# Token rows loaded ahead of the last prefetched weight tiles, and narrow products as four 32-token strips

## What is computed

```
# block 1, layer l: the segment ab of the input projection, 4*8 = 32 columns
h = rmsnorm(x, norm_w[l]);  proj = h @ w_in[l]       # ab: decay and gate of the 8 heads
# block 2
x = x + mix @ w_out
hf = rmsnorm(x, g_ffn)
logits = hf @ w_router + b_router                    # 256 x 32
top 4 of 32 per token, gates = softmax of the four
for each expert e, on the rows of its tokens (xb):
    gu = xb @ w_gate_up[e] + b_gate_up[e]            # 1024 x 2048
    g = min(gu[:, :1024], 7);  u = clip(gu[:, 1024:], -7, 7)
    y = ((u + 1) * g * sigmoid(1.702 g)) @ w_down[e] + b_down[e]
x = x + sum of y * gate
gate = sigmoid(rmsnorm(x, g_ple) @ w_ple_gate)
x = x + (p @ w_ple_proj) * gate                      # p: 256 tokens x 256
out = rmsnorm(x, g_final)
```

## Time and profile before

| | us |
|---|---|
| median of three runs | 2119.19 |
| the three runs | 2116.81, 2119.19, 2123.26 |
| the profiled execution, its own time | 2117.58 |
| its span, first to last instruction | 2115.7 |
| TensorE busy | 2011.1 (95%) |
| VectorE busy | 718.4 (34%) |
| ScalarE busy | 449.7 (21%) |
| GpSimdE busy | 100.7 (5%) |

### The profile page before, as it was taken

How to read it: one execution, slowest core, us unless ns; L and a number is a source line. 1 busy time by engine, 2 the same in 40 slices (tenths; PEclk the granted TensorE clock), 3 DMA queues, 4 the chain that set the end, 5 groups by cost and what they waited for, 6 DMA issues and landing times.

```text
span 2115.7 us, 24433 instructions
## 1 busy us (share of the span) xinstructions
PE 2011.1 (95%) x9554; PEld 986.8 (47%) x9554; DVE 718.4 (34%) x2021; ACT 449.7 (21%) x1121; POOL 100.7 (5%) x84
## 2 busy tenths in 40 slices
PE   7999999999999999999996999999999999999998
PEld 6754666445864566544463333333333333333334
DVE  4659565211767666311143111111101111011112
ACT  2151554211143355310121000000000000000003
POOL 0021220000022121000000000000000000000000
PEclk9999999998999999999997999999999999999999
DMA  6643212343453221344816999999999999999993
GB/s 213 251 147 120 81 41 81 120 159 119 145 213 120 83 78 41 119 159 172 305 53 249 387 428 428 427 429 428 429 428 429 428 428 429 427 430 428 429 426 113
DMA packets 103070, 551.17 MB, mean 261 GB/s; under 512 B 9005, under 2 KB 13521, under 8 KB 77906
## 3 DMA queue, kind: packets, MB, share of 16 engines
q1 hardware_dynamic: 101138, 549.57, 64.6%
q10 hardware_dynamic: 1856, 0.57, 0.1%
HBM read 546.90 MB, written 3.21 MB: 260 GB/s over the span
## 4 chain that ended last, share of the span: by engine, by line
PE 75%; DMA 18%; DVE 4%; issue 1%; ACT 1%; SPq 0%; DVEq 0%; ACTq 0%
PE bank L570 26%; PE bank L1111 13%; DMA ring<-w_gate_up_dram 8%; DMA region<-w_gate_up_dram 8%; PE bank L1137 7%; PE bank L856 5%; PE bank L909 3%; PE bank L682 3%; PE bank L1069 2%; PE bank L1055 2%; PE bank L993 1%; PE bank L1103 1%; DMA region<-p_dram 1%; PE bank L766 1%; PE bank L822 1%
## 5 line engine op out<-in xcount | busy, mean ns | idle before, releaser
L1111 PE MATMUL bank<-ring,region 128*64 128x512 f32 x1280 | 288.9, 600 | 16.2 <-DMA ring<-w_gate_up_dram 16.2
L2202 DVE TENSOR_SCALAR region<-bank 128x512 f32<-128x512 f32 x32 | 22.1, 691 | 732.3 <-PE bank L1111 732.3
L570 PE MATMUL bank<-ring,hT 128*128 128x512 f32 (+1 forms) x464 | 194.8, 577 | 0.0
L1111 PEld LDWEIGHTS bank<-ring,region 128*64 128x64 f32 x1280 | 88.1, 138 | 215.1 <-issue 177.1
L1111 PE MATMUL bank<-region 128*64 128x512 f32 x768 | 172.2, 595 | 13.5 <-DMA region<-w_gate_up_dram 13.5
L570 PE MATMUL bank<-ring,region 128*128 128x512 f32 x400 | 175.3, 598 | 4.5 <-ACT region L1203 4.5
L570 PE MATMUL bank<-hT,ring 128*128 128x256 f32 x768 | 172.6, 387 | 3.1 <-DMA ring<-w_in_dram 3.1
L570 PEld LDWEIGHTS bank<-hT,ring 128*128 128x128 f32 x768 | 148.3, 194 | 25.8 <-issue 5.0
L1137 PE MATMUL bank<-ring,region 128*64 128x512 f32 x640 | 142.6, 595 | 10.4 <-DVE region L2212 6.9
L570 PEld LDWEIGHTS bank<-ring,hT 128*128 128x128 f32 x464 | 87.5, 190 | 99.9 <-issue 98.5
L1554 ACT ACTIVATE region<-region 128x512 f32<-128x512 f32 x32 | 20.2, 630 | 523.8 <-DVE region L2202 523.8
(11 more groups left out here) (353 smaller groups left out, 2206.1 us busy)
## 6 DMA issues: line engine op xcount, KB each, us to landing
ring<-w_gate_up_dram SPq DMA_DIRECT2D x80, 2048.0 KB, 31.0
region<-w_gate_up_dram SPq DMA_DIRECT2D x48, 2048.0 KB, 32.3
ring<-w_in_dram SPq DMA_DIRECT2D x44, 2048.0 KB, 7.9
ring<-w_down_dram SPq DMA_DIRECT2D x40, 2048.0 KB, 35.3
region<-w_down_dram SPq DMA_DIRECT2D x24, 2048.0 KB, 35.3
ring<-w_out_dram SPq DMA_DIRECT2D x5, 2048.0 KB, 8.2
ring<-rows_scratch SPq DMA_DIRECT2D x4, 2048.0 KB, 9.6
ring<-w_pa_dram SPq DMA_DIRECT2D x4, 2048.0 KB, 7.7
```

The costliest lines, as they stand in the source:

```text
L570: mm = pe.matmul(dst, lhs(k), w(k), start=(k == 0), stop=(k == n_k - 1))
L1111: mm = pe.matmul(pb[g][hf * 64:(hf + 1) * 64, :], XT[:, 2 * (j % 2) + kk, j // 2, :], wj[:, kk, c:c + NB], start=False, stop=(j == 3 and k ...
L2202: dve.tensor_scalar(gm, pb[0][:, :], 7.0, None, ALU.min).then_inc(s("g_clamped"), 1)
```

## The change

Three edits. SyncE issues the load of the token rows as the first after `x_mixed`, with tile 4 behind it and the four small loads. On TensorE the four transposes of the token rows stand behind `turn_gathered`, and so does ScalarE's copy of them behind `turned(1)`. The products with 32 columns (`ab_product` in both layers, the router's logits) go through a new function `narrow`, which splits the 128 tokens of a step into four strips of 32 weight columns, each written to its own 32 partitions of the output. Sums and inputs are the same.

```diff
@@ sync
             sp.wait_ge(s("x_mixed"), 4)
-            expert_tile(4, 0)
+            load(ptok, a["p_2"][0, 0].rearrange("(t p) c -> p t c", p=P), "ple_in")
             load(biases[0:NE, :], a["b_down_2"][0], "bias_in")
             for g in range(2):
                 load(biases[NE * (g + 1):NE * (g + 2), :], a["b_gate_up_2"][0, :, g * D:(g + 1) * D], "bias_in")
             load(one_of, a["c_one_of"], "bias_in")
-            for T in range(5, 8):
+            for T in range(4, 8):
                 expert_tile(T, T // 6)
-            load(ptok, a["p_2"][0, 0].rearrange("(t p) c -> p t c", p=P), "ple_in")
             for T in range(8, 6 * GROUP):
@@ tensor
+            def narrow(dst, lhs, w):
+
+                for k in range(KC):
+                    for c in range(0, P, 32):
+                        mm = pe.matmul(dst[c:c + 32, :], lhs(k)[:, c:c + 32], w(k), start=(k == 0), stop=(k == KC - 1))
+                return mm
+
@@ ab_product
-                        mm = product(pb[6][:, t * 32:(t + 1) * 32], lambda k: hT[:, k, t * P:(t + 1) * P],
+                        mm = narrow(pb[6][:, t * 32:(t + 1) * 32], lambda k: hT[:, k, t * P:(t + 1) * P],
                                      lambda k: wab[:, l * 256 + k * 32:l * 256 + (k + 1) * 32])
@@ router
-                mm = product(pb[0][:, t * NE:(t + 1) * NE], lambda k: hT[:, k, t * P:(t + 1) * P], lambda k: wr[:, k, :])
+                mm = narrow(pb[0][:, t * NE:(t + 1) * NE], lambda k: hT[:, k, t * P:(t + 1) * P], lambda k: wr[:, k, :])
@@ before expert 0
             gather()
+            pe.wait_ge(s("X_sb"), 1)
+            turn_gathered()
             pe.wait_ge(s("ple_in"), 16)
             for t in range(NT):
                 for k in range(2):
                     mm = pe.transpose(pb[2][:, k * S + t * P:k * S + (t + 1) * P], ptok[:, t, k * P:(k + 1) * P], ident)
             mm.then_inc(once("pT_ps"), 1)
-            pe.wait_ge(s("X_sb"), 1)
-            turn_gathered()
@@ scalar
             gathered(1)
+            turned(1)
             await_once(act, "pT_ps")
             act.activation(pT, pb[2][:, :].rearrange("p (k t) -> p k t", k=2), ACT.Copy).then_inc(once("pT_sb"), 1)
-            turned(1)
```

## The result

The changed kernel takes 2098.5 us (median of four runs, 2092.24 to 2101.25) against 2118.09 for the kernel before (median of four): the ratio is 0.9905, with a 95% interval of 0.989 to 0.992. Five more runs of it later had a median of 2098.76. The profiled execution took 2098.96 us with a span of 2097.1, 18.6 us less than the span before.

The account below looks back on a forecast made before the run. TensorE was taken to bound the first half and the weight-tile stream the second; -8.7 (part 1) + 0.4 (layer 0) - 1.8 (layer 1) + 0 (router) = -10.1 us, from 2119.19 to 2109.1 us, range 2103 to 2114.5.

Parts of the forecast that it names:

- The bound: Second half: the weight-tile stream at 428 GB/s sets the time, only an earlier start counts; before about 1115 us, TensorE.
- Part 1: Token rows loaded before tile 4, their transposes behind the turn: bias products start at 1135.6 instead of 1144.27, 8.7 us earlier.
- The router: Router's logits: VectorE reads them only behind its scaling of the rows, so a shorter product gives 0, a longer one costs.
- The price of a strip: Narrow products: 29 ns for each of 128 records, 3.9 us a product; +0.4 us in layer 0, -1.8 in layer 1.
- the rival of full overlap: Narrow products: strips side by side take 1.3 us a product, total 2103.9 us, or 2102.2 if the clock returns sooner; 18%.
- The clock in layer 1: Wide products behind layer 1's narrow product: the clock may come back sooner or not, worth 0 to 1.7 us.
- The clock in expert 0: From the bias products on: half clock may last longer or shorter after an earlier start, 1.7 us either way.

Follow-up runs that it names:

- part 1 alone: Kernel before with the token rows loaded first and their transposes and ScalarE's copy behind the turn, narrow products full-width: 2107.21 us, ratio 0.9956.
- the load first: Kernel before with only the token rows' load moved ahead of tile 4, old order on TensorE, narrow products full-width: 2104.07 us, ratio 0.994.
- The tile with one and with two groups: Changed kernel plus unread products behind the router's: 32-column strips in one column group, 32 ns each; 64-column strips in two groups, 29 ns each.
- the strips in layer 1: Kernel before with only layer 1's narrow product split into strips of 32 weight columns: 2113.32 us, ratio 0.9982.
- the series of 512: Kernel before with layer 1's narrow product in strips and done four times over, 512 records: 2128.91 us, ratio 1.0056.

## Why the prediction was wrong

**The bound: right.** The stream of weight tiles sets the second half, and what starts it earlier is won to the end: behind expert 0 the difference of the two traces doesn't move any more.

**Part 1: right, in place and size.** -8.7 forecast, -8.85 measured; -8.7 in the trace of part 1 alone. The load landed after 3.1 us, the bias products followed the transposes, and of the 13 us of standstill some 3 stayed. The move on TensorE, which the forecast costed together with the load, carries none of it: with the load early the old order is as good, and with the load late it brings 1.3 us in the trace.

**The router: right in these traces.** A shorter product gives 0. From its start to the ranking products it takes 8.98 us before (1117.60 to 1126.58) and 8.99 after (1108.63 to 1117.62), though the product is 2.7 us shorter: VectorE's scaling (L1623) is late in both. It is closer than "0" says: where the clock falls during the full-width product, as in part 1 alone, that product ends behind the scaling and costs 0.7. And it may have cost something: from the start of the router's product to the end of expert 0's gate and up products the changed kernel gained 9.7 us, part 1 alone 12.3 and the load first 12.6, both with the full-width product and with the clock back before the bias products, not 5.5 us behind their start. The shorter product leaves TensorE a wait of 7.70 us in place of 4.5 to 5. No run has the change without the router's strips, so whether they cost these 3 us isn't shown.

**The price of a strip: wrong, and the larger part of the miss.** The step was "I take 29 ns, the row with the nearest tile and the same moving columns". It measured 9.6 ns. In layer 0 that is -2.2 and not +0.4, in layer 1 -4.5 and not -1.8, together 5.3 us. The row was near in its tile but its pace came from its 64-column weight loads in two groups; the prediction gave this scaling (7 to 9 ns) as the lower bound and as the rival of full overlap. The tile with one and with two groups confirms it. A row's number should be carried over only with what sets it. By the prediction's own rows wide records move 512 columns in 431 ns, 27 ns for 32, so the 109 ns of a full-width record with 32 moving columns weren't the moving.

**The clock in layer 1: right in kind, too small.** "worth 0 to 1.7 us" was 2.85: the clock didn't come back sooner, it never fell. The prediction took the low clock as given and asked when it ends. It should have asked whether it starts. What makes it start stays open.

**The clock in expert 0:** -0.8 of the 1.7 allowed either way; in part 1 alone and the load first it was 3.6, outside of them. Elsewhere the low clock near 483 us went and one near 976 came, -1.6 and +1.7. They cancel here; the second comes with the strips in layer 1, as the table of the windows shows.

Together: 5.3 + 2.85 + 0.8 + 0.15 (part 1) less 0.4 (the start) and 0.1 are 8.6 us, the difference between -10.1 and the -18.6 of the traces but for rounding. The case that came true is the full overlap of the strips, which had 18%. Its gain was 15.3 us, or 17 with the clock, against 19.6 measured; its times of 2103.9 and 2102.2 were too high by a further 1.1, as they were counted from 2119.19 and the median before is 2118.09 with the fourth run. The range ended at 2103 and so left out the case of full overlap with its clock.

The rule of the Trainium skill that spoke against the strips ("TensorEngine Tiling (Array Packing)", "Instruction Overhead") was not borne out for a series of 128 records: 9.6 ns each, far below its 60 cycles, which would be 25 ns at the full 2.4 GHz (an estimate). The other rule weighed, that a weight load overlaps a running matmul only for another row group ("TensorE: Matmul & The Clock Gate", "The mechanism"), doesn't hold for these strips either: all four use the same 128 rows, and four of them take 35 ns where a strip alone in its column group takes 32.

## What to carry to other kernels

A product with few moving columns runs at the pace of its weight load, so cutting the weight columns into strips with output partitions of their own (four of 32, or two of 64) takes it down to a third or to half, as long as the series is short: 128 records ran without a gap here, and 512 didn't. Where another engine is late anyway, as at the router, a shorter product only makes the wait longer. Before a stage that sets the time, look at TensorE's granted clock as at any other cost: a wait that is hidden behind another engine can still halve the speed of the products that follow, and wide products that nobody reads can help once no longer wait stands behind them. A trace of one execution shows where the clock fell in it and not where it falls: compare the same windows in all traces, those of unchanged parts too, before a gain is put down to an edit. A small load that an engine needs early belongs ahead of the large ones in its queue; here that alone gave all of its part.

## What the runs showed of the hardware

- Strips of 32 weight columns in four column groups start 8.7 ns apart in float32 at the full clock (13.3 ns at half, in the later bursts of the series of 512), 32 ns in one group, 29 ns for 64 columns in two; full-width records 109 ns.
- A series of 512 such records came in bursts, 167 and then 128 at most, with waits of 1.5 to 4.7 us, each later burst 2.4 to 2.5 us behind the start of a 16 KB instruction packet; 31.7 ns a record in the mean.
- A load of 256 KB landed 3.1 us after its issue ahead of the tiles of 2 MB and 22.5 us behind them, on the same queue.
- The clock fell to half in stretches in which TensorE was never idle (75 to 95 us: granted 0.83 in the traces of part 1 alone and of the strips in layer 1, 1.00 in that of before). Executions of one kernel differ by it: the changed kernel's four runs have granted clocks of 0.995 at 2092.24 us and 0.989 at 2101.25.
